# A third block of the down-projection by seven block products, in a two-layer encoder on one core

## The chip, the cores and the metric

One core of a Trainium2 chip runs the whole program. Its engines are TensorE (PE, matrix products, with its own weight loads, PEld), VectorE (DVE), ScalarE (ACT), GpSimd (POOL) and SyncE (SP), which issues the transfers. The metric is device time in microseconds; the time given is the median of three runs. A page of the profile and its trace come from one execution.

## The reference

Two layers of a streaming encoder work on 640 frames (512 of a prompt, 128 of a sample) of width 1024: a norm, an input projection, two groups of attention heads, an output projection, and then the feed-forward part that the change is about. All is float32.

```python
def swiglu(x, g, w_gate, w_up, w_down):
    n = rms_norm(x, g)
    return (jax.nn.silu(n @ w_gate) * (n @ w_up)) @ w_down

xp = xp + swiglu(xp, ffn_norm[l], w_gate[l], w_up[l], w_down[l])
...
y_prompt = rms_norm(xp, final_norm)
```

The hidden width is 2816, that is 22 tiles of 128.

## The kernel before, in words

**Products in three parts.** A float32 product is made of a high and a low part of each side: high by high, low by high and high by low, so that each product of 128 by 128 weights with 320 columns costs three matmuls (lines 1359 to 1361). Everything is held transposed, features on the partitions and the 640 frames in two halves of 320 columns: x as `xT` in 8 chunks.

**Seven products for eight.** A 2x2 block product can be made by seven block products of sums of the blocks. The kernel takes two output tiles of weights together with the two halves of frames as such blocks. Each group n has seven products x = 1 to 7; the left sides are sums of weight blocks (`left_sums`, L2481, DVE), split into a high part (`left_high`, L1879, ACT) and a low one (`left_low`, L2503, DVE) in a ring of six buffers. The order is the list `RUN` (L122). ACT works five products ahead (`HIGH_AHEAD`), DVE four (`AHEAD`): step i of DVE's loop is the sum and the low part for product i + 4, then what empties the banks of product i (`emptied`, L2551).

**The feed-forward part.** Tiles 0 to 3 of the hidden width go plainly. Tiles 4 to 21 are nine pairs: an even group n makes gate, an odd one up, so n = 0 to 17, seven products of 12 matmuls each. The down-projection sums over the hidden tiles in four blocks: 0 (tiles 0 to 3), 1, 2 and 3 (six tiles each). Blocks 1 and 2 go by block products too: four groups for each block (n = 18 to 25), seven products of 9 matmuls, 252 for a block, each group giving two chunks of `xT`. `emptied` calls `down_emptied` (L2530) for these: one addition from PSUM into `xT` for each product (L2543). The right sides are sums of hidden blocks, whose high parts ACT makes (`down_right_hi`, L1893) and whose low parts DVE makes (`down_right_lo`, L2509).

**Rows.** Blocks 0 and 3 (`ROWS_IN_PLACE`, L65) go plainly: for each of 8 output chunks d the weight tile is loaded (`load_down`, L630), split by ACT (`weight_hi`, L1471) and DVE (`weight_lo`, L2034), multiplied (`down_rows`, L1364; 36 matmuls in block 3, so 288 in all), and added into `xT` (L2715). The pairs of block 3 keep plain right sides for that (`in_rows`, L1905; `hidden_lo`, L2444). In block 3's rows a chunk is finished after each d: ACT squares it (L1469), POOL adds the square into `ssq` for the next norm (`sum_squares`, L2749), and ACT and DVE make the next layer's normed input `nh` and `nl` (L1467, L2041), or, in layer 1, `yT`.

**Between the layers** the input projection of layer 1 takes its weights in units u of 512 KB, through the same two buffers as the rows (`load`, L521). PE waits for `x_new` first (L711).

**The program's end** (L1413 to 1456): the last output chunk is made in two parts of 256 and 384 columns (`last_rows`); matmuls of one column sum `ssq` over the partitions, `y_turn` (L685) transposes `yT` tile by tile, ACT and DVE scale by the root into `yout` (L2008, L2722), and SP sends it out.

## Time and profile before

| what | us |
|---|---|
| median of 3 runs (1427.94 to 1428.9) | 1428.51 |
| the profiled execution | 1429.83 |
| its span | 1428.54 |
| PE busy in it | 1402.7 |
| rows of block 3, layer 0 | 42.38 |
| rows of block 3, layer 1, to the last data matmul | 44.89 |
| from there to the end | 8.99 |

The span runs from the first to the last record; 1.3 us of the profiled execution lie around it. A busy share is a mean over all stages; what an edit is worth is read in the stage where it stands.

### The profile page before, as it was taken

To read this page: it belongs to the slowest core of one execution; us is meant where nothing else is said; L and a number is where in the kernel's file an instruction comes from. 1 tells how busy PE (TensorE), PEld (TensorE's weight loads), DVE (VectorE), ACT (ScalarE), POOL (GpSimd) and SP (SyncE) were. 2 spreads that over 40 slices of the span, in tenths; PEclk is the share of its full clock that TensorE was granted. 3 is DMA by queue.
4 is the path that set the end of the run, shared out by engine and by line. 5 is a ranking of instruction groups with operands and counts; after the bars stand their busy time and mean duration, and the time that the engine had idled before them with its cause. 6 is when DMAs were issued, how large, how long until landed. Compare 5 with 4: busy or idle time off the path is not lost.

```text
span 1428.5 us, 24281 instructions
## 1 busy us (share of the span) xinstructions
PE 1402.7 (98%) x9340; PEld 1321.5 (93%) x9340; DVE 1061.1 (74%) x1875; ACT 713.0 (50%) x1414; POOL 156.6 (11%) x110
## 2 busy tenths in 40 slices
PE   7999999999999999999999999999999999999998
PEld 6897878999999999999988978699999999999998
DVE  5658667878789889877444776677797998998853
ACT  5458555334355455454444685643344544544534
POOL 2416020210000000000222341102000000000002
PEclk9999999999999999999999999999999999999999
DMA  5330221233022222322233211213221223222312
GB/s 171 109 113 14 74 70 39 81 104 104 30 89 66 89 84 74 104 89 74 74 84 107 85 56 47 77 42 102 79 74 60 82 71 114 62 88 89 111 45 96
DMA packets 148642, 115.25 MB, mean 81 GB/s; under 512 B 17936, under 2 KB 143248, under 8 KB 148496
## 3 DMA queue, kind: packets, MB, share of 16 engines
q1 hardware_dynamic: 148528, 113.71, 26.4%
q8 instruction: 75, 1.23, 0.4%
q14 instruction: 39, 0.32, 0.1%
HBM read 108.90 MB, written 6.62 MB: 81 GB/s over the span
## 4 chain that ended last, share of the span: by engine, by line
PE 86%; DVE 7%; ACT 3%; DMA 1%; issue 1%; SPq 1%; DVEq 0%; ACTq 0%
PE ps L675 23%; PE ps L1359 13%; PE ps L1360 13%; PE ps L1361 13%; PE ps L802 3%; PE ps L804 3%; PE ps L803 3%; PE ps L1236 1%; PE ps L1127 1%; ACT pw L1521 1%; PE ps L728 1%; DMA wraw<-w_uq 1%; DVE ringl L2507 1%; PE ps L917 1%; PE ps L1153 1%
## 5 line engine op out<-in xcount | busy, mean ns | idle before, releaser
L2037 DVE TENSOR_TENSOR wlo<-wraw,whi 128x1024 fp32r<-128x1024 f32 (+2 forms) x87 | 97.6, 1122 | 122.9 <-ACT whi L1475 122.8
L1360 PE MATMUL ps<-tl,ringh 128*128 128x320 f32 x576 | 177.8, 309 | 0.0
L1361 PE MATMUL ps<-tth,ringl 128*128 128x320 f32 x576 | 177.5, 308 | 0.0
L1359 PE MATMUL ps<-tth,ringh 128*128 128x320 f32 x576 | 177.0, 307 | 0.0
L1891 ACT ACTIVATE ringh<-sums 128x512 fp32r<-128x512 f32 (+1 forms) x208 | 123.7, 595 | 106.3 <-DVE sums L2499 35.9
L2507 DVE TENSOR_TENSOR ringl<-sums,ringh 128x512 fp32r<-128x512 f32 (+1 forms) x208 | 134.2, 645 | 9.6 <-ACT ringh L1891 8.2
L1475 ACT ACTIVATE whi<-wraw 128x1024 fp32r<-128x1024 f32 (+2 forms) x87 | 81.0, 936 | 112.5 <-PE ps L675 52.0
L1360 PE MATMUL ps<-tbl,ringh 128*128 128x320 f32 x432 | 133.5, 309 | 0.0
L1361 PE MATMUL ps<-tbh,ringl 128*128 128x320 f32 x432 | 133.4, 309 | 0.0
L1359 PE MATMUL ps<-tbh,ringh 128*128 128x320 f32 x432 | 133.4, 309 | 0.0
L1359 PE MATMUL ps<-dhi,ringh 128*128 128x320 f32 x336 | 105.6, 314 | 5.2 <-DVE dlo_rest L2512 2.8
L1359 PEld LDWEIGHTS ps<-tth,ringh 128*128 128x128 f32 x576 | 108.2, 188 | 0.0
L1361 PEld LDWEIGHTS ps<-tth,ringl 128*128 128x128 f32 x576 | 108.2, 188 | 0.0
L1360 PEld LDWEIGHTS ps<-tl,ringh 128*128 128x128 f32 x576 | 108.0, 187 | 0.0
L1361 PE MATMUL ps<-dhi,ringl 128*128 128x320 f32 x336 | 103.8, 309 | 0.0
L2755 POOL TENSOR_TENSOR ssq<-sq 128x640 f32<-128x640 f32 x4 | 6.5, 1628 | 886.1 <-ACT sq L1469 886.1
L1360 PE MATMUL ps<-dlo_rest,ringh 128*128 128x320 f32 x288 | 89.0, 309 | 0.0
L802 PE MATMUL ps<-whi,nh 128*128 128x512 f32 (+1 forms) x220 | 86.4, 393 | 0.7 <-DVE nl L2041 0.7
L804 PE MATMUL ps<-whi,nl 128*128 128x512 f32 (+1 forms) x220 | 84.0, 382 | 0.0
L803 PE MATMUL ps<-wlo,nh 128*128 128x512 f32 (+1 forms) x220 | 83.8, 381 | 0.0
L1359 PEld LDWEIGHTS ps<-tbh,ringh 128*128 128x128 f32 x432 | 81.1, 188 | 0.0
L1361 PEld LDWEIGHTS ps<-tbh,ringl 128*128 128x128 f32 x432 | 81.1, 188 | 0.0
(431 smaller groups left out, 3786.4 us busy)
## 6 DMA issues: line engine op xcount, KB each, us to landing
raw_gate<-w_gate SPq DMA_DIRECT2D x18, 1024.0 KB, 5.4
raw_up<-w_up SPq DMA_DIRECT2D x18, 1024.0 KB, 5.3
raw_gate<-w_down SPq DMA_DIRECT2D x8, 768.0 KB, 4.2
raw_up<-w_down SPq DMA_DIRECT2D x8, 768.0 KB, 4.2
wraw<-w_down SPq DMA_DIRECT2D x16, 384.0 KB, 3.3
wraw<-w_out SPq DMA_DIRECT2D x32, 128.0 KB, 2.9
wraw<-w_out SPq DMA_DIRECT2D x16, 256.0 KB, 3.1
wraw<-w_gate SPq DMA_DIRECT2D x8, 512.0 KB, 3.9
```

The source lines that it names most:

```text
L675: ins = mm(outs[j], wt[:, k, cols], x[:, half(j)], start=first and part == 0 and x is xh, stop=last and part == 1)
L728: ins = turn(ps[:, 5 + b % 3, j * P:(j + 1) * P], src, ident)
L802: mm(o, nh[:, c, tok(t)], wh[:, k, 0:w], start=c == 0, stop=False)
L803: mm(o, nh[:, c, tok(t)], wl[:, k, 0:w], start=False, stop=False)
L804: ins = mm(o, nl[:, c, tok(t)], wh[:, k, 0:w], start=False, stop=c == NC_ - 1)
L1359: mm(o, wh[:, c, :], xh[:, c, :], start=fresh and c == 0, stop=False, skip_group_check=True)
L1360: mm(o, wh[:, c, :], xl[:, c, :], start=False, stop=False, skip_group_check=True)
L1361: ins = mm(o, wl[:, c, :], xh[:, c, :], start=False, stop=c == (DP if down else KH) - 1, skip_group_check=True)
L1475: run(whi[:, unit_cols(u)], wraw[:, unit_cols(u)], ACT.Copy).then_inc(unit_hi.sem, 1)
L1891: run(ring_of(n, x)[0], left_of(n, x), ACT.Copy).then_inc(a_hi.sem, 1)
L2037: vec.tensor_tensor(wlo[:, w], wraw[:, w], whi[:, w], ALU.subtract).then_inc(unit_lo.sem, 1)
L2507: vec.tensor_tensor(lo, left_of(n, x), high, ALU.subtract).then_inc(a_lo.sem, 1)
```

## The change

In both layers block 3's down-projection goes by seven block products as well (`NDOWN` 3 x 4 groups, n = 18 to 29): 252 matmuls in place of 288. Its rows, their loads and splits, and the `in_rows` case of pairs 6 to 8 leave; those pairs make right sides like the others. The very last group (n = 29) takes its products in the order 1, 5, (28, 4), 6, 2, 7, 4, 3.

`first_rights` puts two low parts of right sides ahead of the sum and the low part in DVE's step.

ACT squares chunks in pairs at step 6 of groups 27, 28 and 29 (and makes `yT` there in layer 1), and POOL adds them there. The next layer's first two weight units have buffers of their own, in space that is free once the last gate and up group is done; the third is loaded when all products of the layer are done. `nh` and `nl` follow when the ring's buffers are free.

At the program's end, twelve turns of `yT` stand between the last products of PE; the rest of the turns and the square sums (three matmuls of one column for a tile) follow the last product.

The diff, cut to what the text speaks of:

```diff
-NDOWN = 2 * KH
+NDOWN = 3 * KH
...
-ROWS_IN_PLACE = (0, 3)
-UNITS = U_DOWN + len(ROWS_IN_PLACE) * NC_
+UNITS = U_DOWN + NC_
...
+        yield n, 2
+        yield n, 7
 
 
 def down_products(blk):
@@ -114,12 +108,11 @@
         yield n, 5
         yield (n - 1 if n > first else GROUPS_OF[blk][1] - 1), 4
         yield n, 6
-        yield n, 3
-        yield n, 2
-        yield n, 7
-
-
-RUN = [key for part in (products(1), down_products(1), products(2), down_products(2), products(3)) for key in part]
+        for x in (3, 2, 7) if n < NG + NDOWN - 1 else (2, 7, 4, 3):
+            yield n, x
+
+
+RUN = [key for part in (products(1), down_products(1), products(2), down_products(2), products(3), down_products(3)) for key in part]
...
+def row_done(d):
+
+    n = NG + 2 * KH + d // 2
+    return D_NEW[n, 4] if d % 2 else max(D_NEW[n, 2], D_NEW[n, 3])
...
+    _, next_raw, next_hi, next_lo = place(R0, [("skip_next", [P, 2560], F32), ("next_raw", [P, 2 * SLOT], F32),
+                                               ("next_hi", [P, 2 * SLOT], F32R), ("next_lo", [P, 2 * SLOT], F32R)])
...
-    yT, = place(20480, [("yT", [P, NC_, T], F32)])
+    yT, = place(R0 + 20480, [("yT", [P, NC_, T], F32)])
...
+                if l and u == 0:
+                    sp.wait_ge(a_used.sem, a_used.at(l - 1, STEP[NG - 1, 4] + 1))
+                if l and u == 2:
+                    sp.wait_ge(a_used.sem, a_used.at(l, 0))
...
-            sp.wait_ge(a_used.sem, a_used.at(l, STEP[NG + NDOWN - 1, 4] + 1))
-            for d in range(NC_):
-                load_down(3, d)
...
-            if l > 0:
-                pe.wait_ge(x_new.sem, x_new.at(l, -1))
...
+                        if l and u == 0 and k == 0 and t in (0, 3):
+                            pe.wait_ge(d_new.sem, d_new.at(l - 1, D_NEW[NG + NDOWN - 2, 4] if t == 0 else NDOWN * 7))
...
+                if l == DEPTH - 1 and n == NG + NDOWN - 1 and x == 7:
+                    pe.wait_ge(n_hi.sem, n_hi.at(DEPTH, -3))
+                    y_turn(0, range(4))
+                    pe.wait_ge(d_new.sem, d_new.at(l, D_NEW[n - 1, 4]))
+                    y_turn(1, range(4))
+                if l == DEPTH - 1 and n == NG + NDOWN - 1 and x == 4:
+                    pe.wait_ge(n_hi.sem, n_hi.at(DEPTH, -1))
+                    for t in range(2):
+                        y_turn(t, range(4, 6))
...
+            y_turn(t, range(6, 8)).then_inc(tile_turned.sem, 1)
...
+            ins = square_sums(2, t, [ssq, sq[:, 0], sq[:, 1]])
...
+        y_turn(2, range(6))
+        pe.wait_ge(n_hi.sem, n_hi.at(DEPTH, 1))
+        pe.wait_ge(y_gained.sem, 2)
+        y_turn(2, range(6, 8)).then_inc(tile_turned.sem, 1)
+        pe.wait_ge(sq_new.sem, sq_new.at(DEPTH, 3))
         for t in range(2, NT):
-            mm(ps[:, 7, 500 + t:501 + t], ssq[:, tok(t)], one, start=t == 2, stop=False, skip_group_check=True)
-        pe.wait_ge(y_gained.sem, 2)
-        y_turn(2, range(7, 8)).then_inc(tile_turned.sem, 1)
-        pe.wait_ge(sq_new.sem, sq_new.at(DEPTH, 2))
-        for t in range(2, NT):
-            ins = mm(ps[:, 7, 500 + t:501 + t], sq[:, 1, tok(t)], one, start=False, stop=True, skip_group_check=True)
+            ins = square_sums(3, t, [ssq, sq[:, 0], sq[:, 1]])
...
+            def squared(c):
+
+                act.wait_ge(d_new.sem, d_new.at(l, row_done(c)))
+                act.wait_ge(ssq_new.sem, ssq_new.at(l, 14 + adds_before(c)))
+                run(sq[:, c % 2, :], xT[:, c, :], ACT.Square).then_inc(sq_new.sem, 1)
+
+            def gained(c, cols=slice(0, T)):
+
+                act.wait_ge(d_new.sem, d_new.at(l, row_done(c)))
+                run(yT[:, c, cols], xT[:, c, cols], ACT.Copy, scale=gv[:, G_NEXT + c:G_NEXT + c + 1]).then_inc(n_hi.sem, 1)
+
+            def next_high(c):
+
+                act.wait_ge(d_new.sem, d_new.at(l, row_done(c)))
+                act.wait_ge(a_used.sem, a_used.at(l, min(len(RUN), len(RUN) - 4 + c)))
+                run(nh[:, c, :], xT[:, c, :], ACT.Copy, scale=gv[:, G_NEXT + c:G_NEXT + c + 1]).then_inc(n_hi.sem, 1)
+
+            for i, (n, x) in enumerate(RUN):
+                if i + HIGH_AHEAD < len(RUN):
+                    left_high(*RUN[i + HIGH_AHEAD])
+                elif i + HIGH_AHEAD < len(RUN) + 2 and l < DEPTH - 1:
+                    weight_hi(l + 1, i + HIGH_AHEAD - len(RUN))
+                emptied(n, x)
+                if x == 6 and n > NG + 2 * KH:
+                    for c in (2 * (n - NG - 2 * KH) - 2, 2 * (n - NG - 2 * KH) - 1):
+                        if l == DEPTH - 1:
+                            gained(c)
+                        squared(c)
+            if l < DEPTH - 1:
+                for c in range(NC_ - 1):
+                    next_high(c)
+                squared(NC_ - 2)
...
-                if g == 0 and x == 6:
-                    down_right_lo(q, 5, 3, 4, tu[:, 1:2, half(0)])
...
+            def first_rights(n, x):
+
+                if n >= NG and (n - NG) % KH == 0 and x == 6:
+                    down_right_lo(DP * ((n - NG) // KH) + DP - 1, 5, 3, 4, tu[:, 1:2, half(0)])
+                elif n < NG and n % 2 and x == 7:
+                    down_right_lo(n // 2, 1, 0, 1, tu[:, 0:1, half(0)])
...
-                    if up and not in_rows:
+                    if up:
                         dve.wait_ge(c_new.sem, c_new.at(l, C_NEW[n, 3]))
                         dve.wait_ge(silu_new.sem, silu_new.at(l, PLAIN + SILU[2 * pair, 2]))
                         chain("b12", vec.tensor_tensor(tu[:, 0, half(1)], tu[:, 0, half(1)], tg[:, 0, half(1)], ALU.mult))
@@ -2581,9 +2579,6 @@
                     if up:
                         dve.wait_ge(c_new.sem, c_new.at(l, C_NEW[n, 2]))
                         dve.wait_ge(silu_new.sem, silu_new.at(l, PLAIN + SILU[2 * pair, 2]))
-                    if up and in_rows:
-                        vec.tensor_tensor(tu[:, 0, :], tu[:, 0, :], tg[:, 0, :], ALU.mult).then_inc(h_new.sem, 1)
-                    elif up:
                         vec.tensor_tensor(tu[:, 0, half(0)], tu[:, 0, half(0)], tg[:, 0, half(0)], ALU.mult).then_inc(h_new.sem, 1)
                         chain_end("b12")
                         dve.wait_ge(h_new.sem, h_new.at(l, PLAIN + pair + 1))
@@ -2595,9 +2590,7 @@
                         else:
                             chain("t1", t1)
                 elif x == 7:
-                    if up and not in_rows:
-                        down_right_lo(pair, 1, 0, 1, tu[:, 0:1, half(0)])
...
-                    if in_rows:
-                        hidden_lo(f, tu[:, 0, :])
-                    elif not final:
+                    if not final:
                         down_right_lo(pair, 2, 1, 3, t12[:, :, :])
                     dve.wait_ge(a_used.sem, done)
                     dve.wait_ge(silu_new.sem, silu_new.at(l, PLAIN + SILU[2 * pair, 4]))
                     vec.tensor_tensor(tu[:, 1, half(0)], ps[:, bx, 0:HALF], tg[:, 1, half(0)], ALU.mult).then_inc(up_c21.sem, 1)
-                    if not in_rows:
-                        dve.wait_ge(right_new.sem, right_new.at(l, right_sums_before(pair) + 1 + final))
-                        dve.wait_ge(up_c21.sem, up_c21.at(l, pair + 1))
-                        vec.tensor_tensor(t34[:, 1, :], tu[:, 1, half(0)], t12[:, 1, :], ALU.subtract).then_inc(right_new.sem, 1)
-                elif x == 6 and not up and pair > 2 * DP:
-                    hidden_lo(f - 1, tu[:, 1, :])
+                    dve.wait_ge(right_new.sem, right_new.at(l, right_sums_before(pair) + 1 + final))
+                    dve.wait_ge(up_c21.sem, up_c21.at(l, pair + 1))
+                    vec.tensor_tensor(t34[:, 1, :], tu[:, 1, half(0)], t12[:, 1, :], ALU.subtract).then_inc(right_new.sem, 1)
...
+            def next_low(c):
+
+                dve.wait_ge(n_hi.sem, n_hi.at(l, 9 + c + 1))
+                if c < 2:
+                    dve.wait_ge(a_used.sem, a_used.at(l, len(RUN) - 2 + c))
+                low(nl[:, c, :], xT[:, c, :], gv[:, G_NEXT + c:G_NEXT + c + 1], nh[:, c, :]).then_inc(n_lo.sem, 1)
+
+            def gained_part(c, cols):
+
+                dve.wait_ge(d_new.sem, d_new.at(l, D_NEW[NG + NDOWN - 1, 4 if c == 7 else 3]))
+                vec.tensor_scalar(yT[:, c, cols], xT[:, c, cols], gv[:, G_NEXT + c:G_NEXT + c + 1], None, ALU.mult).then_inc(y_gained.sem, 1)
+
+            for i, (n, x) in enumerate(RUN):
+                first_rights(n, x)
+                if i + AHEAD < len(RUN):
+                    left_sums(*RUN[i + AHEAD])
+                    left_low(*RUN[i + AHEAD])
+                elif l < DEPTH - 1:
+                    if i + AHEAD < len(RUN) + 2:
+                        weight_lo(l + 1, i + AHEAD - len(RUN))
+                    else:
+                        next_low(i + AHEAD - len(RUN) - 2)
+                emptied(n, x)
+                if l == DEPTH - 1 and n == NG + NDOWN - 1 and x == 4:
+                    gained_part(7, slice(0, CUT))
+            if l < DEPTH - 1:
+                for c in range(2, NC_ - 1):
+                    next_low(c)
+            else:
+                gained_part(6, slice(CUT, T))
...
-            sum_squares(l, ssq, 18, 14, NC_ - 1)
+            sum_squares(l, ssq, 18, 14, NC_ - 1 if l < DEPTH - 1 else NC_ - 2)
```

## Rows read from the trace of the kernel before

**Rows 1.** Page: busy us (share of span) x instructions; PE clock in 40 slices.

```profile
PE 1402.7 (98%) x9340; PEld 1321.5 (93%) x9340; DVE 1061.1 (74%) x1875; ACT 713.0 (50%) x1414; POOL 156.6 (11%) x110
...
PEclk9999999999999999999999999999999999999999
```

**Rows 2.** Chain of waits: start, us, engine, tile, line, count.

```profile
676.86 42.23 PE ps L675 x288
...
1374.82 36.95 PE ps L675 x252
```

**Rows 3.** Windows: us; busy PE PEld DVE ACT POOL; clock, DMA share, GB/s.

```profile
448.46:492.70 44.24, 43.11 (x291) 42.23 (x290) 41.44 (x90) 19.04 (x39) 0.00 (x0) 1.00 0.31 99
...
492.70:561.23 68.53, 68.53 (x471) 68.53 (x469) 58.67 (x106) 37.51 (x73) 0.00 (x0) 1.00 0.24 75
...
561.23:606.41 45.18, 43.38 (x291) 42.24 (x289) 41.38 (x90) 19.33 (x39) 0.00 (x0) 1.00 0.31 98
...
1260.34:1304.57 44.23, 43.10 (x290) 42.22 (x289) 41.45 (x90) 19.12 (x39) 0.00 (x0) 1.00 0.31 100
```

**Rows 4.** Chain of waits, a transfer after 561.23.

```profile
573.66 6.41 DMA raw_gate<-w_down
```

**Rows 5.** Page, DMA issues: count, size, us to landing.

```profile
raw_gate<-w_down SPq DMA_DIRECT2D x8, 768.0 KB, 4.2
```

**Rows 6.** Windows of the first down stage, in two parts.

```profile
446.14:473.20 27.06, 25.93 (x173) 25.05 (x173) 26.68 (x60) 11.19 (x24) 0.00 (x0) 1.00 0.27 88
...
473.20:487.85 14.65, 14.65 (x102) 14.65 (x101) 13.29 (x30) 5.62 (x11) 0.00 (x0) 1.00 0.23 73
```

**Rows 7.** Timeline of PE: start, us, operation, [idle before <- releaser].

```profile
449.90 0.42 PE L1359 MATMUL ps<-dhi,ringh 128*128 128x320 f32 x1 [0.42 <-DVE dlo_first L2512]
...
457.98 0.41 PE L1359 MATMUL ps<-dhi,ringh 128*128 128x320 f32 x1 [0.69 <-DVE dlo_rest L2512]
```

**Rows 8.** Lines of DVE, 446:487: count | busy us, mean ns | idle.

```profile
L2543 DVE TENSOR_TENSOR xT<-ps,xT 128x320 f32<-128x320 f32 x26 | 12.6, 484 | 1.4 <-PE ps L1361 1.4
...
L2507 DVE TENSOR_TENSOR ringl<-sums,ringh 128x384 fp32r<-128x384 f32 x15 | 8.2, 550 | 0.0
```

**Rows 9.** Windows of block 3's rows in both layers, and the end.

```profile
676.70:719.08 42.38, 42.38 (x291) 42.16 (x289) 21.05 (x24) 17.55 (x23) 9.90 (x6) 1.00 0.22 63
...
1374.66:1419.55 44.89, 44.89 (x315) 44.82 (x314) 14.78 (x20) 19.65 (x28) 9.39 (x6) 1.00 0.13 36
...
1419.55:1428.54 8.99, 4.18 (x37) 3.81 (x35) 3.88 (x7) 3.03 (x6) 0.00 (x0) 0.97 0.73 292
```

**Rows 10.** Lines of ACT in layer 0's rows stage.

```profile
L1469 ACT ACTIVATE sq<-xT 128x640 f32<-128x640 f32 x7 | 5.1, 723 | 0.0
```

**Rows 11.** Timelines of POOL and DVE at two places.

```profile
716.25 1.65 POOL L2755 TENSOR_TENSOR ssq<-ssq,sq 128x640 f32<-128x640 f32 x1 [1.83 <-ACT sq L1469]
...
717.15 1.83 DVE L2037 TENSOR_TENSOR wlo<-wraw,whi 128x1024 fp32r<-128x1024 f32 x1 [0.69 <-ACT whi L1475]
...
721.80 1.23 DVE L2037 TENSOR_TENSOR wlo<-wraw,whi 128x1024 fp32r<-128x1024 f32 x1
...
282.44 1.65 POOL L2755 TENSOR_TENSOR ssq<-ssq,sq 128x640 f32<-128x640 f32 x1 [4.33 <-ACT sq L1469]
...
284.00 0.81 DVE L2433 TENSOR_TENSOR xt<-ps,rB 128x640 f32<-128x640 f32 x1
```

**Rows 12.** Timelines of the program's end, runs of one line together.

```profile
1420.36 0.83 PE L1445 MATMUL ps<-kc,ssq 128*128 128x1 f32 x6
...
1421.78 1.94 PE L689 MATMUL ps<-kc,yT 128*128 128x128 f32 x16
...
1422.47 2.07 DVE L2724 TENSOR_SCALAR yout<-ps,small 128x512 f32<-128x512 f32 x3
...
1424.61 0.33 SPq L655 DMA_DIRECT2D out_ys<-yout  x1
```

**Rows 13.** DMA issues after layer 0's rows, input weights.

```profile
wraw<-w_in SPq DMA_DIRECT2D x4, 512.0 KB, 3.6
```

More of the change, by code:

```diff
@@ L1413, in last_rows @@
-        def last_rows(right, rows):
-            wh, wl = unit_parts(UNITS - 1, P)
-            cols = slice(CUT, T) if right else slice(0, CUT)
-            out = ps[:, 6 + right, 0:cols.stop - cols.start]
-            for f in rows:
-                mm(out, wh[:, f, :], hh[:, f, cols], start=f == 0, stop=False)
-                mm(out, wh[:, f, :], hl[:, f, cols], start=False, stop=False)
-                ins = mm(out, wl[:, f, :], hh[:, f, cols], start=False, stop=f == TILES[-1] - 1)
-            return ins
@@ new lines, in _ @@
+            for n, x in RUN:
+                product(n, x)
+                if l == DEPTH - 1 and n == NG + NDOWN - 1 and x == 7:
[7 more added lines that the diff above has]
+                        y_turn(t, range(4, 6))
@@ new lines, in _ @@
+            for d in range(NC_):
+                if d == 0:
+                    right_high_sums(3)
+                if d + 6 < NC_:
+                    weight_hi(l, U_DOWN + d + 6)
+                if 2 <= d < 2 + HIGH_AHEAD:
+                    left_high(*RUN[d - 2])
+            def squared(c):
+                act.wait_ge(d_new.sem, d_new.at(l, row_done(c)))
+                act.wait_ge(ssq_new.sem, ssq_new.at(l, 14 + adds_before(c)))
+                run(sq[:, c % 2, :], xT[:, c, :], ACT.Square).then_inc(sq_new.sem, 1)
@@ L2597, in emptied @@
                 elif x == 7:
[L2598 to L2600 removed]
+                    if up and final:
                         down_right_lo(pair, 2, 1, 2, t12[:, 0:1, :])
@@ L2608, in emptied @@
                         b22 = vec.tensor_tensor(tu[:, 1, half(1)], tu[:, 1, half(1)], tg[:, 1, half(1)], ALU.mult)
-                    if up and not in_rows:
                         chain("b22", b22)
@@ new lines, in _ @@
+            weight_lo(l, U_DOWN + 2)
+            hidden_lo(PLAIN - 1, tu[:, 1, :])
+            right_low_plain(2)
+            weight_lo(l, U_DOWN + 3)
+            right_low_sums(2)
+            right_rows(3)
+            weight_lo(l, U_DOWN + 4)
+            right_sums(3)
+            weight_lo(l, U_DOWN + 5)
+            right_low_plain(3)
+            for d in range(NC_):
+                if d == 2:
+                    right_low_sums(3)
+                if d in (2, 3):
+                    weight_lo(l, U_DOWN + d + 4)
+                if 2 <= d < 2 + AHEAD:
+                    left_sums(*RUN[d - 2])
+                    left_low(*RUN[d - 2])
+                b0 = 2 * DOWN_PAIR[d]
+                dve.wait_ge(unit_used.sem, unit_used.at(l, U_DOWN + d + 1))
+                vec.tensor_tensor(halves(xT[:, d, :]), ps[:, b0:b0 + 2, 0:HALF], halves(xT[:, d, :]), ALU.add).then_inc(x_new.sem, 1)
```

278 lines of the change are left out of this document (82 added, 196 removed).

## Prediction

> **What bounds the kernel.** I read the busy times first, then the granted clock, then the chain of waits. TensorE (PE) is busy 98% of the span, with the granted clock at its upper level, 2.4 GHz, in all 40 slices [rows 1]. So a change is worth what it takes from PE's own work, less the waits that it puts before PE. In the chain the plain down-projection of block 3 is one run of PE in each layer: 42.23 us for 288 matmuls in layer 0, that is 0.1466 us for one of 320 columns; layer 1's 252 in one run take 36.95, the same each [rows 2]. The stage windows show what seven block products cost in practice. A gate and up stage of block products takes 68.53 us for its 468 matmuls, 0.1464 each: nothing waits there, though VectorE (DVE) is busy 58.67 of it. A down stage (36 matmuls of the group before, 252 of its own) takes 44.24, 45.18 and 44.23 in the three windows shown [rows 3]; 288 x 0.1465 is 42.2. So each loses 2.0 us, and 45.18 once. That 0.95 more is one late transfer, 6.41 us against the usual 4.2 [rows 4, 5].
>
> **Why a down stage loses 2 us** is seen on DVE: in its first 27 us it is busy 26.68 of 27.06, and in the next 14.65 it has 1.36 free [rows 6]. PE's stalls name it: 0.42 for dlo_first and 0.69 for dlo_rest, the low parts of the right side [rows 7]; behind each comes some 0.1 to refill. A group of seven products brings DVE 7 lows and 4 sums at 0.55 and 7 additions into xT at 0.48 [rows 8]; the sums have the shape of the lows. They overlap at their ends, so that they start some 0.47 and 0.40 apart: 11 x 0.47 + 7 x 0.40 = 8.0 of the 9.23 us that PE needs for 63 matmuls. In the rows stage that the change replaces, DVE is busy 21.05 of 42.38 [rows 9]: half free.
>
> **The method for the new stages.** Each engine takes its queue in order, so I walked the four queues operation by operation: one starts when its engine is free and its last wait is met, with the durations of the rows. For the old down stages this gives 44.1 against the 44.24 of the window: an error of 0.1 in a stage. The order stands in RUN: DVE does the sums and the low of the product four ahead, then xT for the present one.
>
> **Part 1, the products.** 36 matmuls fewer per layer: 252 x 0.1465 = 36.92 in place of 42.38, that is -5.4 before any wait. Entry to the new stage: DVE is as full as in the other two, 2.15 by the walk (2.03 measured). Pairs 6 to 8 now make right sides as the others do; block 3's gate and up stage becomes the one that waited for nothing [rows 3], so 0. On SP's queue eight loads of 384 KB leave in each layer and eight of 768 KB for two groups each come; each has the lead of the ring as now (4.2 us), so 0, and 0.95 for each that is late as in [rows 4].
>
> **Part 2, the square sums.** This is what decides. In the rows stage ScalarE squares each finished chunk (0.72) and POOL adds it into ssq (1.65) [rows 10, 11], beside a half idle DVE. Now both come in pairs inside the product stage: at step 6 of groups 27, 28 and 29, five adds in a layer. ScalarE has the room. POOL's adds are another thing: the weight low part at 717.15 took 1.83, with an add running from 716.25 for 1.65, and 1.23 right after, alone. The difference is about what was left of the add. An operation that reads PSUM, at 284.00, took its 0.81 while an add was ending [rows 11]. So I take it that an operation of DVE with both inputs in SBUF (lows, sums, weight lows) stands until the add is over, and xT, which reads PSUM, does not. The Trainium skill says this in its page "SBUF — State Buffer", section "SBUF: two separate sides": the port pair that GpSimd and DVE share is an exclusive lock for a whole instruction, against DVE operations with two SBUF inputs. By that rule the walk below holds, and without it the first rival; the row at 717.15 agrees (0.60 longer), but no row shows it with DVE full.
>
> Layer 0, by the walk with these holds: adds 1 to 3 hold lows of groups 27 to 29 for 0.95, 1.40 and 1.00; DVE's slack of 1.2 us in a group doesn't win that back, and product 4 of group 28 waits 0.93 for xT of its product 7. Adds 4 and 5 then hold the two weight lows of the next layer, 1.00 each. Those two (1.23 each) now stand in DVE's queue just before xT of product 7 of the last group, for which product 4 waits. The queue is: weight low 0, xT of product 2, weight low 1, xT of product 7; PE stands 3.58 there (1.10 without the holds). Sum: 36.92 + 2.15 + 0.93 + 3.58 + 0.2 for two refills = 43.8, against 42.38: **+1.4**. Without the holds 36.92 + 3.36 = 40.3: -2.1.
>
> Layer 1 has no weight lows there, but ScalarE makes yT there too: product 4 of group 27 waits 1.27 and of group 28 1.57 (all excess over 36.92, turns included, is 6.6; without the holds 4.4). Twelve turns of yT stand between the last products, 0.12 each by the 16 turns in 1.94 [rows 12]: 1.4. Sum to the last product's end: 36.92 + 2.15 + 1.27 + 1.57 + 0.2 + 1.4 = 43.5.
>
> **Part 3, the program's end.** Now: 8.99 from the last data matmul to the end, of which 5.06 to the last output's issue at 1424.61 and 3.93 after it [rows 9, 12]. After: xT of the last product 0.75 behind its end, square and yT of that part 0.6, then 15 one-column sums and the turns of tile 2 (six sums took 0.83) until 3.05; root and reciprocal until 3.7, three yout in 2.07, issue and transfer 3.93: **9.7**. So layer 1 from the start of the stage is 43.5 + 9.75 = 53.3 against 44.89 + 8.99 = 53.9: **-0.6**. Without holds -2.8.
>
> **Part 4, smaller steps.** first_rights puts two low parts ahead of a sum and a low in DVE's step. With DVE full this only moves which operation is late: by the walk 0 to +0.24 in each of the four old stages (the stalls of [rows 7] go, and others come at products 6 and 7, for xT). The other bound is that the stalls go: -1.1 for each. I take +0.15, the walk being within 0.1 of what is measured: **+0.6**. The next layer's first two weights have buffers of their own and come 20 us ahead: 0. The third is asked for after the last product; it lands 3.6 us later [rows 13], ScalarE and DVE need some 2.3 for it (1.23 the low part), and PE has two units of thirty 512-column matmuls first, 7 us each by 512/320 of 0.1466. So some 3 us are left when ScalarE waits for the first unit to be used: 0; without that cover it would cost what it is late. Normed chunks of the next layer: the first two lows end within 0.3 of PE's last product: 0 to +0.3, taken 0.
>
> **Sum**: +1.4 - 0.6 + 0.6 = +1.4. The profiled execution took 1429.83, 1.32 above the median of 1428.51; 0.95 of that is the late transfer, which I don't expect again. Against its own time 1429.83 - 0.95 + 1.4 = 1430.3; against the median 1429.9. I take the latter, as three runs carry it.
>
> **Rivals.** (A) The adds don't hold DVE in this stage, or fall beside xT and idle ends: -2.1 - 2.8 + 0.6 = -4.3, 1424.2. For it: the profile's durations of POOL are rough, the holds are seen at few places, and DVE has no full stage with adds in the trace. Against: 717.15. (B) Slower: the holds reach PE in full. Each of the eight adds that have two-input operations beside them (five in layer 0, three in layer 1, where the last two come after the last low) holds DVE 1.4 us, 11.2 in all, and DVE, with 1.36 free in 14.65, makes none of it up. The place is product 4 of groups 27 to 29. Layer 0: 36.92 + 3.36 + 7.0 - 42.38 = +4.9; layer 1: 36.92 + 4.4 + 4.2 + 9.75 - 53.9 = +1.4; with +0.6 it is +6.9, 1435.4. In the forecast 5.7 of the 11.2 reach PE; above 7.2 the change is slower by over 0.2%. For it: POOL may be held by DVE in turn, so that adds end later and a square waits for its buffer, and left_high stands behind it on ScalarE. (C) first_rights does remove the entry stalls, in all six stages: 6 x -1.1 in place of the +0.6, with the holds of the forecast: 1.4 - 0.6 - 6.6 = -5.8, 1422.7. Against: DVE 99% busy at entry [rows 6].
>
> **How the numbers follow.** Forecast 0.50, A 0.21, C 0.05, B 0.24. About 0.2%, 2.86 us, is what a measurement tells from no change: faster is under 1425.65, slower over 1431.37. A and C are faster (0.26), the forecast within (0.50), B slower (0.24). The range leaves out C and B's upper half: 1423.6 (A with a little less in the entries) to 1433.5 (half of B's 5.5 us on top of the forecast, and one late transfer). The forecast's own range is 1427.5 to 1432.3.
>
> **What would show it.** Right: PE in both new stages with 252 matmuls in 37 us of work and 5 to 7 us of stalls, the largest before product 4 of the last group in layer 0, released by xT; lows and weight lows of 1.4 to 2.2 us beside POOL's adds; old down stages at 44.2 to 44.5. Wrong: lows of 0.55 beside adds (A); old down stages near 43 (C); a stall before product 4 of every group of over 2 us (B); a wait of PE for the third weight unit, which I hold at 0.

## The result, and the profile after

| | us |
|---|---|
| before, median of 7 runs (1427.45 to 1428.9) | 1427.94 |
| after, median of 7 runs (1430.48 to 1435.95) | 1432.93 |
| ratio, 95% interval | 1.0037, 1.0026 to 1.0047 |
| profiled execution after | 1433.07 |
| its span | 1431.8 |

The changed kernel is 5.0 us slower, 0.35%. PE has less to do, as meant (1398.7 us busy against 1402.7 in [rows 1]), and waits more. The windows of the changed kernel show where (length; busy time of PE, PEld, DVE, ACT, POOL; granted clock; DMA share; GB/s): the first down stage of layer 0, the last of layer 0 with block 3, one old stage of layer 1, the last of layer 1, and the end.

```profile
447.12:491.44 44.32, 43.06 (x290) 42.22 (x289) 41.54 (x90) 19.29 (x39) 0.00 (x0) 1.00 0.31 100
672.65:719.16 46.51, 41.43 (x266) 40.04 (x265) 44.17 (x84) 22.91 (x42) 9.20 (x5) 0.96 0.22 73
1261.98:1306.65 44.67, 43.35 (x291) 42.23 (x289) 41.48 (x90) 19.36 (x39) 0.00 (x0) 1.00 0.31 98
1375.18:1419.91 44.73, 41.42 (x278) 39.99 (x277) 37.92 (x81) 25.58 (x49) 8.36 (x5) 1.00 0.16 52
1419.91:1431.77 11.86, 8.06 (x60) 7.66 (x57) 4.92 (x9) 4.70 (x9) 0.00 (x0) 0.84 0.56 223
```

These answer to [rows 3] and [rows 9]. The new stages start 12 matmuls (1.76 us) earlier than the rows did, since product 4 of the last up group now stands inside them. So 46.51 is to be held against 42.38 + 1.76 = 44.14, and 44.73 against 44.89 + 1.76 = 46.65. In the 42.38 of [rows 9] DVE was busy for half the time and the clock stood at 1.00; now it is busy 44.17 of 46.51, and the clock's mean is 0.96.

| part | before | after | difference | forecast |
|---|---|---|---|---|
| four old down stages, without the late transfer | 176.95 | 177.84 | +0.9 | +0.6 |
| layer 0, last stage | 44.14 | 46.51 | +2.4 | +1.4 |
| layer 1's first units (to the first turn of ssq) | 20.52 | 20.84 | +0.3 | 0 |
| layer 1, last stage | 46.65 | 44.73 | -1.9 | -1.4 |
| the end | 8.99 | 11.86 | +2.9 | +0.8 |
| sum | | | +4.5 | +1.4 |

The sum (4.5 before the parts are rounded) is near the measured 5.0. Single profiles differ in stretches that no edit here touches: in the changed kernel and its nine variants below the first down stage starts anywhere from 445.61 to 449.58. So the experiments are read by these stages first, and by their medians second.

**Layer 0's wait.** The largest wait of the new stages is before product 4 of layer 0's last group. Timelines of POOL, DVE and PE at that place (start, us, operation, and idle time before it with its releaser):

```profile
709.51 4.06 POOL L2743 TENSOR_TENSOR ssq<-ssq,sq 128x640 f32<-128x640 f32 x2 [4.80 <-ACT sq L1957]
...
709.85 2.32 DVE L2032 TENSOR_TENSOR next_lo<-next_raw,next_hi 128x1024 fp32r<-128x1024 f32 x1
712.09 0.48 DVE L2535 TENSOR_TENSOR xT<-ps,xT 128x320 f32<-128x320 f32 x1
712.49 2.16 DVE L2032 TENSOR_TENSOR next_lo<-next_raw,next_hi 128x1024 fp32r<-128x1024 f32 x1
714.58 0.48 DVE L2535 TENSOR_TENSOR xT<-ps,xT 128x320 f32<-128x320 f32 x1
...
715.11 0.64 PE L1353 MATMUL ps<-dhi,ringh 128*128 128x320 f32 x1 [3.49 <-DVE xT L2535]
715.54 0.47 PE L1354 MATMUL ps<-dlo_rest,ringh 128*128 128x320 f32 x1
```

Two adds of POOL run, and beside them the two weight lows of DVE take 2.32 and 2.16 (1.23 alone in [rows 11]), while xT between them takes its 0.48. The xT at 714.58 is the one that PE waits for. The matmul after the wait takes 0.64, the next 0.47, where 0.31 is usual: the granted clock has fallen. Windows of half a microsecond, the last column but two:

```profile
714.00:714.50 0.50, 0.00 (x0) 0.00 (x0) 0.50 (x1) 0.00 (x0) 0.00 (x0) 1.00 0.00 0
714.50:715.00 0.50, 0.00 (x0) 0.00 (x0) 0.50 (x3) 0.00 (x0) 0.00 (x0) 0.62 0.00 0
715.00:715.50 0.50, 0.39 (x1) 0.39 (x2) 0.50 (x2) 0.00 (x0) 0.00 (x0) 0.50 0.00 0
...
718.00:718.50 0.50, 0.50 (x5) 0.50 (x5) 0.50 (x2) 0.50 (x1) 0.00 (x0) 0.96 0.00 0
```

PE had stood idle since 711.6. From 714.6 to 718.0 the clock is at its lower level, 1.2 GHz, over 11 of the last 18 matmuls.

**Layer 1's waits and the end.** Product 4 of groups 27 and 28 waits 1.08 and 1.00, and the end takes PE without a gap from 1419.91 on:

```profile
1400.06 0.41 PE L1353 MATMUL ps<-dhi,ringh 128*128 128x320 f32 x1 [1.08 <-DVE xT L2535]
...
1410.58 0.41 PE L1353 MATMUL ps<-dhi,ringh 128*128 128x320 f32 x1 [1.00 <-DVE xT L2535]
...
1419.91 0.60 PE L683 MATMUL ps<-kc,yT 128*128 128x128 f32 x4
1420.35 0.28 PE L1397 MATMUL ps<-kc,ssq 128*128 128x1 f32 x2
1420.49 0.58 PE L1397 MATMUL ps<-kc,sq 128*128 128x1 f32 x4
...
1422.52 0.28 PE L1397 MATMUL ps<-kc,ssq 128*128 128x1 f32 x2
...
1424.44 3.53 PE L683 MATMUL ps<-kc,yT 128*128 128x128 f32 x16
1424.62 0.27 ACT L2018 ACTIVATE small<-ps,kc 128x3 f32<-128x3 f32 x1 [1.07 <-PE ps L1397]
...
1425.97 0.33 SPq L650 DMA_DIRECT2D out_y<-yout  x1
...
1428.84 0.33 SPq L650 DMA_DIRECT2D out_ys<-yout  x1
```

Each sum of one column is two records: the sums of tiles 2 to 4, nine of them, are 18 records from 1422.52 to 1424.44, 0.107 each and 0.214 for a sum. The root of the last three tiles comes 4.71 after the last product. The last turns run at the lower clock (3.53 for 16, against 1.94 in [rows 12]).

### The profile page after: what moved, and what is told of

Same layout as the page of the kernel before. It is cut to its first block, busy times and chain, and to the rows that moved or that the text cites. A ratio compares the mean times of both kernels' runs of the same rounds, so it can differ in the third digit from the quotient of the medians.

```text
span 1431.8 us, 24544 instructions
## 1 busy us (share of the span) xinstructions
PE 1398.7 (98%) x9278; PEld 1314.9 (92%) x9278; DVE 1124.8 (79%) x2032; ACT 732.1 (51%) x1472; POOL 157.6 (11%) x109
## 3 DMA queue, kind: packets, MB, share of 16 engines
q8 instruction: 75, 1.23, 0.4%
## 4 chain that ended last, share of the span: by engine, by line
PE 80%; DVE 12%; ACT 3%; issue 3%; DMA 1%; SPq 1%; DVEq 0%; ACTq 0%
PE ps L670 18%; PE ps L1353 13%; PE ps L1354 13%; PE ps L1355 13%; PE ps L796 3%; PE ps L798 3%; PE ps L797 3%; DVE ringl L2501 2%; DVE xT L2535 2%; PE ps L1230 1%; PE ps L1121 1%; ACT pw L1487 1%; PE ps L720 1%; PE ps L911 1%; PE ps L1147 1%
## 5 line engine op out<-in xcount | busy, mean ns | idle before, releaser
L1353 PE MATMUL ps<-dhi,ringh 128*128 128x320 f32 x504 | 159.5, 317 | 13.4 <-DVE xT L2535 13.0
L2501 DVE TENSOR_TENSOR ringl<-sums,ringh 128x512 fp32r<-128x512 f32 (+1 forms) x240 | 152.6, 636 | 7.9 <-ACT ringh L1857 6.4
L1355 PE MATMUL ps<-dhi,ringl 128*128 128x320 f32 x504 | 156.2, 310 | 0.0
L2032 DVE TENSOR_TENSOR wlo<-wraw,whi 128x1024 fp32r<-128x1024 f32 (+1 forms) x69 | 79.3, 1149 | 79.4 <-ACT whi L1442 79.3
L1354 PE MATMUL ps<-dlo_rest,ringh 128*128 128x320 f32 x432 | 133.9, 310 | 0.0
L1442 ACT ACTIVATE whi<-wraw 128x1024 fp32r<-128x1024 f32 (+1 forms) x69 | 65.8, 956 | 93.6 <-PE ps L798 38.2
L1353 PEld LDWEIGHTS ps<-dhi,ringh 128*128 128x128 f32 x504 | 95.1, 189 | 20.1 <-DVE xT L2535 19.7
L1355 PEld LDWEIGHTS ps<-dhi,ringl 128*128 128x128 f32 x504 | 95.1, 189 | 0.0
L2535 DVE TENSOR_TENSOR xT<-ps,xT 128x320 f32<-128x320 f32 x168 | 82.2, 490 | 14.9 <-PE ps L1355 14.9
L1354 PEld LDWEIGHTS ps<-dlo_rest,ringh 128*128 128x128 f32 x432 | 81.7, 189 | 0.0
```

Of the source, the lines that this page charges most:

```text
L1353: mm(o, wh[:, c, :], xh[:, c, :], start=fresh and c == 0, stop=False, skip_group_check=True)
L1354: mm(o, wh[:, c, :], xl[:, c, :], start=False, stop=False, skip_group_check=True)
L1355: ins = mm(o, wl[:, c, :], xh[:, c, :], start=False, stop=c == (DP if down else KH) - 1, skip_group_check=True)
L1442: run(high[:, unit_cols(u)], raw[:, unit_cols(u)], ACT.Copy).then_inc(unit_hi.sem, 1)
L2032: vec.tensor_tensor(lo[:, w], raw[:, w], high[:, w], ALU.subtract).then_inc(unit_lo.sem, 1)
L2501: vec.tensor_tensor(lo, left_of(n, x), high, ALU.subtract).then_inc(a_lo.sem, 1)
```

## The experiments

The theory had three parts: POOL's adds hold DVE's operations with two inputs in SBUF; in layer 0 the weight lows stand before the xT that PE waits for; and, new from the trace after, the clock falls behind that wait and at the end. The rivals: DVE's queue is simply full, with or without adds; the clock costs nothing; and the reordering of the right sides is to blame.

The kernel before was timed again beside each series: 1427.94 beside the changed kernel; 1428.42 beside the short adds, the fillers, the lows behind and the old right sides; 1427.29 beside the late squares, the pieces and the first order of the end; 1428.44 beside the last two. The changed kernel was not, so a difference from its median of about 1 us says nothing.

### The adds cut short

```diff
-                first = sq[:, 0, :] if c == 1 else into[:, :]
-                add(into[:, :], first, sq[:, c % 2, :], ALU.add).then_inc(ssq_new.sem, 1)
+                w = slice(0, 8 if squares_before == 18 else T)
+                first = sq[:, 0, w] if c == 1 else into[:, w]
+                add(into[:, w], first, sq[:, c % 2, w], ALU.add).then_inc(ssq_new.sem, 1)
```

> The changed kernel with POOL's adds of squares in the last product stage cut from 640 columns to 8, so that sums of squares are left out for most columns; every wait stands as it was. Theory (an add of POOL holds DVE's operations with two inputs in SBUF): DVE's weight lows take 1.23 in place of 2.2 to 2.3; the wait before product 4 of the last group in layer 0 falls from 3.65 to about 1.1 us and the clock stays up; layer 1's waits before product 4 of groups 27 and 28 (1.24 and 1.16) mostly go. Layer 0 about 4 us less, layer 1 about 2: 1427. Rival (DVE's queue is full by itself): the waits stay, 1433.

This kernel leaves out most of the sums of squares. Measured: 1426.70 (11 runs), 0.9985 of before (0.9977 to 0.9994) and 6.2 us under the changed kernel. Windows of the two last stages and of the end:

```profile
671.53:713.58 42.05, 39.80 (x266) 38.70 (x265) 39.45 (x84) 23.18 (x42) 1.40 (x5) 1.00 0.23 79
1369.95:1412.61 42.66, 41.41 (x278) 40.00 (x277) 35.86 (x81) 25.55 (x49) 1.13 (x5) 1.00 0.17 55
1412.61:1424.47 11.86, 6.47 (x60) 6.24 (x57) 4.73 (x9) 4.58 (x9) 0.00 (x0) 0.90 0.56 223
```

DVE at the same place as above, and PE's wait:

```profile
707.64 1.22 DVE L2032 TENSOR_TENSOR next_lo<-next_raw,next_hi 128x1024 fp32r<-128x1024 f32 x1
708.77 0.48 DVE L2535 TENSOR_TENSOR xT<-ps,xT 128x320 f32<-128x320 f32 x1
709.17 1.21 DVE L2032 TENSOR_TENSOR next_lo<-next_raw,next_hi 128x1024 fp32r<-128x1024 f32 x1
...
710.84 0.41 PE L1353 MATMUL ps<-dhi,ringh 128*128 128x320 f32 x1 [1.01 <-DVE xT L2535]
```

The weight lows take 1.22 and 1.21. Layer 0's last stage loses 4.46 us, layer 1's 2.07, and the clock stays at 1.00 in both. So the adds, not a queue that is full anyway, cost 6.5 us in the changed kernel, a part of it by way of the clock (the next experiment); only about 1 us of the wait in layer 0 is the queue's own. This is the size of rival A of the prediction in both layers (-2.1 for the first stage: 42.05 against 44.14; for layer 1's, 41.3 worked out without the holds and 42.66 - 1.76 = 40.9 measured). The end is as long as in the changed kernel, 11.86.

### The clock: PE kept at work

```diff
+            def filler(bank, count):
+                key = (NG + NDOWN - 1, 3)
+                pe.wait_ge(a_lo.sem, a_lo.at(l, STEP[key] + 1))
+                for _ in range(count):
+                    mm(ps[:, bank, 0:HALF], ring_of(*key)[0][:, 0, :], dhi[:, RIGHT_OF[3], 0, :], start=True, stop=True, skip_group_check=True)
...
+                if l < DEPTH - 1 and n == NG + NDOWN - 1 and x == 7:
+                    filler(7, 24)
...
         pe.wait_ge(sq_new.sem, sq_new.at(DEPTH, 3))
+        filler(3, 4)
```

> The changed kernel with 24 filler matmuls of 320 columns into an unused bank ahead of the wait of product 4 of the last group in layer 0, and 4 fillers ahead of the last square sums at the program's end. Their results are read by nothing. Theory (the granted clock): the trace after shows the clock at 0.50 behind PE's wait of 3.65 us in layer 0 (714.6 to 718.1) and from 1424.6 at the end, where the last 16 turns take 3.53 us against 1.94 before. With PE at work in both places it stays at 1.00: layer 0's last products take 2.6 us in place of 4.0 (1.1 less to the next layer's start), the turns about 2.0 (1.6 less, 0.6 more for the fillers themselves). In all 2 us less than the changed kernel, 1431. Rival (the clock falls whatever PE does there, or costs nothing): the same 3.5 us of turns, and 0.6 more, 1433.5.

Measured: 1432.81 (7 runs), ratio 1.0033 (1.0022 to 1.0044): as the changed kernel. The places tell more than the sum. PE in layer 0:

```profile
710.38 3.68 PE L1386 MATMUL ps<-dhi,ringh 128*128 128x320 f32 x24
714.06 0.41 PE L1353 MATMUL ps<-dhi,ringh 128*128 128x320 f32 x1
714.31 0.31 PE L1354 MATMUL ps<-dlo_rest,ringh 128*128 128x320 f32 x1
```

Windows of layer 0's last stage, of the end, and of the last turns within it:

```profile
671.51:716.81 45.30, 43.64 (x291) 42.26 (x290) 44.12 (x84) 22.86 (x42) 9.23 (x5) 1.00 0.22 74
...
1418.56:1431.03 12.47, 7.07 (x64) 6.83 (x62) 4.73 (x9) 4.58 (x9) 0.00 (x0) 0.90 0.54 212
1423.50:1425.00 1.50, 1.50 (x15) 1.50 (x16) 0.81 (x2) 0.90 (x3) 0.00 (x0) 1.00 1.02 407
```

In layer 0 the fillers fill the wait, the clock stays at 1.00, and the stage is 1.2 us shorter than the changed kernel's 46.51, as expected (1.1). At the end the clock stays up as well through the last turns (1423.5 to 1425.0), yet the end takes 12.47 in place of 11.86: the 0.6 of the four fillers is paid, and nothing comes back for the clock. The short adds settle the end without fillers: there the clock is at 1.00 until PE's last turn is over, and the end takes the same 11.86. So the fall of the clock costs 1.2 us in layer 0 and nothing at the end. In this profile layer 1's last stage was 45.98 against 44.73, through a longer wait before product 4 of group 28; why it differs from execution to execution was not settled.

### The weight lows behind

```diff
-                    if i + AHEAD < len(RUN) + 2:
-                        weight_lo(l + 1, i + AHEAD - len(RUN))
-                    else:
-                        next_low(i + AHEAD - len(RUN) - 2)
+                    if i == len(RUN) - 2:
+                        weight_lo(l + 1, 0)
+                    if i >= len(RUN) - 2:
+                        next_low(i - len(RUN) + 2)
                 emptied(n, x)
...
             if l < DEPTH - 1:
+                weight_lo(l + 1, 1)
                 for c in range(2, NC_ - 1):
                     next_low(c)
```

> The changed kernel with the next layer's two weight lows moved in DVE's queue: the first behind xT of product 7 of the last group, the second behind the last xT. The adds stay. Theory (what PE waits for is the order of DVE's queue, lengthened by the adds): product 4 of the last group waits under 0.5 us, the clock stays up; the first weight low is then late for the next layer by up to 1.5 us, as it and two lows of the normed chunks stand before PE's next start. In all 3 us less, 1430. Rival (what is won comes back at the next layer's start, with PE waiting there 4 us or more): 1433 or above.

Measured: 1430.45 (11 runs), 1.0012 (1.0003 to 1.0020), 2.5 under the changed kernel. Layer 0's last stage:

```profile
673.53:715.75 42.22, 40.12 (x266) 38.72 (x265) 40.71 (x82) 22.85 (x42) 8.39 (x5) 1.00 0.23 79
```

DVE's first weight low, and what PE waits before product 4:

```profile
712.86 1.80 DVE L2032 TENSOR_TENSOR next_lo<-next_raw,next_hi 128x1024 fp32r<-128x1024 f32 x1
...
713.00 0.42 PE L1353 MATMUL ps<-dhi,ringh 128*128 128x320 f32 x1 [0.58 <-DVE xT L2535]
```

The adds still run, the first low is still held (1.80), but xT is ahead of it: 0.58 of waiting, no fall of the clock, 4.3 us less in the stage. Some 0.3 comes back in the next layer's first unit, where PE waits for a low. Of the 4.0 that are left the median shows 2.5, or 3.0 when each kernel is held against the kernel before of its own series; the rest was not found. What PE waited for was the order; the adds made it long.

### The squares late

```diff
-                if x == 6 and n > NG + 2 * KH:
+                if l == DEPTH - 1 and x == 6 and n > NG + 2 * KH:
                     for c in (2 * (n - NG - 2 * KH) - 2, 2 * (n - NG - 2 * KH) - 1):
...
                 for c in range(NC_ - 1):
                     next_high(c)
-                squared(NC_ - 2)
+                for c in range(NC_ - 1):
+                    squared(c)
```

> The changed kernel with layer 0's squares and POOL's adds behind the last product and the normed chunks, instead of in the product stage; layer 1 stays. Theory (the adds hold DVE in the full stage): layer 0's last stage takes about 42 us in place of 46.5, as with the short adds (42.05), with a wait of 1.2 before product 4 of the last group and the clock at 1.00; layer 1 as in the changed kernel. In all 1428.5. Rival (the holds only move: the adds then hold the lows of the normed chunks, and PE waits in the next layer's first units): 4 us come back there, 1432.5.

Measured: 1433.44 (6 runs), 1.0038 (1.0025 to 1.0051): nothing gained. The stage:

```profile
674.98:717.04 42.06, 39.81 (x267) 38.70 (x265) 39.28 (x84) 19.87 (x36) 0.00 (x0) 1.00 0.23 80
```

ACT, and then PE, in the next layer's first units:

```profile
729.16 0.74 ACT L1957 ACTIVATE sq<-xT 128x640 f32<-128x640 f32 x1 [0.98 <-POOL ssq L2744]
...
731.46 1.99 ACT L1442 ACTIVATE whi<-wraw 128x1024 fp32r<-128x1024 f32 x2
...
734.07 0.50 PE L796 MATMUL ps<-whi,nh 128*128 128x512 f32 x1 [2.87 <-DVE wlo L2033]
```

The stage has the 42.06 of the theory. The rival's time came true by another way than it named: on ACT the squares wait for the adds, two buffers for seven squares, and the third weight unit's high part stands behind them until 731.46; its low part then runs beside POOL's next add. PE waits 2.87 and the clock falls again. What a step waits for moves with it, and so does what is queued behind it.

### The right sides where they were

```diff
-                first_rights(n, x)
...
+                if g == 0 and x == 6:
+                    down_right_lo(q, 5, 3, 4, tu[:, 1:2, half(0)])
                 dve.wait_ge(a_used.sem, a_used.at(l, STEP[n, x] + 1))
...
                 elif x == 7:
+                    if up:
+                        down_right_lo(pair, 1, 0, 1, tu[:, 0:1, half(0)])
```

> The changed kernel with the two low parts of right sides where they were in the kernel before (behind the sum and the low part of DVE's step). Theory (moving them only moves the wait, with DVE full): the stages of blocks 1 and 2 at 44.24 as before in place of 44.3 to 44.7, the entry of block 3's stage alike: 0.6 to 1 us less, 1432. Rival (the move removes the entry waits and something else lengthens these stages): 1 us more for each of six stages, up to 1439.

Measured: 1433.36 (8 runs), 1.0031 (1.0020 to 1.0042): not to be told from the changed kernel. Windows of an old stage in each layer:

```profile
447.67:491.90 44.23, 43.12 (x290) 42.24 (x289) 41.43 (x90) 19.41 (x39) 0.00 (x0) 1.00 0.31 101
1264.64:1308.88 44.24, 43.13 (x290) 42.24 (x289) 41.44 (x90) 19.01 (x39) 0.00 (x0) 1.00 0.31 99
```

44.23 and 44.24 as before, against 44.32 with the reordering: 0.08 for a stage, a half of my 0.15, and far from the -1.1 of rival C. The stages of 44.67 to 44.82 that either order has hold a wait for a late transfer (5.80 us in the changed kernel's chain of waits, at 1274.50; 6.06 and 6.05 here, at 572.86 and 1163.92); the changed kernel's 44.53 has no such transfer in its chain, and its 0.2 more was not explained.

### The adds in pieces, and then everything

The pieces are of 128 columns, so that one fits beside an xT of DVE.

```diff
-                first = sq[:, 0, :] if c == 1 else into[:, :]
-                add(into[:, :], first, sq[:, c % 2, :], ALU.add).then_inc(ssq_new.sem, 1)
+                for t in range(NT if squares_before == 18 else 1):
+                    w = tok(t) if squares_before == 18 else slice(0, T)
+                    first = sq[:, 0, w] if c == 1 else into[:, w]
+                    ins = add(into[:, w], first, sq[:, c % 2, w], ALU.add)
+                ins.then_inc(ssq_new.sem, 1)
```

> The changed kernel with each of POOL's adds in the last product stage cut into five of 128 columns, one after the other. A short add of 8 columns took 0.20 us and one of 640 takes 1.65, so a piece takes about 0.48, little more than an xT (0.40 from start to start), which reads PSUM. Theory (POOL and DVE exclude each other for one instruction at a time): a piece runs under an xT and holds the next low by 0.1 only; the wait before product 4 of layer 0's last group falls from 3.65 to about 1.5, layer 1's two waits from 2.4 to about 1 together: 1428 to 1429.5. Rival (what counts is POOL's time in all, 2.4 us for an add in pieces): the waits stay or grow, 1433 to 1436.

Measured: 1429.39 (11 runs), 1.0012 (1.0003 to 1.0021). Layer 0's last stage:

```profile
672.93:716.09 43.16, 39.88 (x267) 38.73 (x266) 42.20 (x84) 23.09 (x42) 16.16 (x25) 1.00 0.23 78
```

DVE's first weight low, and PE's wait before product 4 of the last group:

```profile
709.57 1.50 DVE L2032 TENSOR_TENSOR next_lo<-next_raw,next_hi 128x1024 fp32r<-128x1024 f32 x1
...
713.34 0.42 PE L1353 MATMUL ps<-dhi,ringh 128*128 128x320 f32 x1 [2.06 <-DVE xT L2535]
```

POOL works 16.2 us in place of 9.2 for the same sums, and the stage is 3.35 us shorter, some 1.2 of it because the clock no longer falls. Here it is the length of one add that counts, not POOL's time in all. In layer 1 it is less plain: its last stage takes 44.36 against 44.73, so the pieces gave back 0.4 of the 2.1 that the short adds gave, and product 4 of groups 27 and 28 still waits 0.57 and 0.86. Why so much less was not followed up. With the weight lows behind as well:

> The changed kernel with POOL's adds in five pieces and, in layer 0, the two weight lows behind the xT that PE waits for. In pieces alone the wait before product 4 of layer 0's last group was 2.2 us, and each weight low took 1.5 there. Theory (the order of DVE's queue and the holds each cost their part of that wait): it falls under 0.5, layer 0's last stage from 43.2 to about 41.8; the next layer's start may wait some 0.4 for its first low. In all 1428.3. Rival (what was won there comes back at the next layer's start): 1429.4.

Measured: 1429.07 (11 runs), 1.0006 (0.9997 to 1.0014); the stage 41.70, as expected, the sum between theory and rival.

```profile
672.21:713.91 41.70, 39.90 (x267) 38.75 (x266) 40.23 (x83) 23.08 (x42) 15.33 (x25) 1.00 0.24 81
```

### The end in another order

First only the sums of tiles 2 to 4 ahead of tile 2's turns:

```diff
         pe.wait_ge(d_new.sem, d_new.at(DEPTH, 0))
-        y_turn(2, range(6))
-        pe.wait_ge(n_hi.sem, n_hi.at(DEPTH, 1))
-        pe.wait_ge(y_gained.sem, 2)
-        y_turn(2, range(6, 8)).then_inc(tile_turned.sem, 1)
         pe.wait_ge(sq_new.sem, sq_new.at(DEPTH, 3))
         for t in range(2, NT):
             ins = square_sums(3, t, [ssq, sq[:, 0], sq[:, 1]])
         ins.then_inc(stat_sum.sem, 1)
+        y_turn(2, range(6))
+        pe.wait_ge(n_hi.sem, n_hi.at(DEPTH, 1))
+        pe.wait_ge(y_gained.sem, 2)
+        y_turn(2, range(6, 8)).then_inc(tile_turned.sem, 1)
```

> The changed kernel with the square sums of tiles 2 to 4 ahead of tile 2's turns at the program's end. The trace after shows PE at work without a gap from the last product's end (1419.91) to 1424.44, and the root of the last three tiles at 1424.62. Theory (PE's one-column sums and turns set the end): the root comes 0.9 earlier, yout of tile 2 waits for its turns until 0.5 earlier than now, and the end is 0.5 earlier: 1432.4. Rival (the output transfers set the end, as they move some 400 GB/s from 1424.0 on): nothing changes, 1432.9.

Measured: 1434.97 (5 runs), 1.0050 (1.0038 to 1.0062). The end is 11.60 in place of 11.86, so the order is worth 0.3; the total is nevertheless the highest of all. In the profile 0.8 us more than in the changed kernel lie in layer 0's last stage, behind a longer fall of the clock (0.94 in place of 0.96), and 1.7 in layer 1 before the feed-forward part:

```profile
671.71:719.06 47.35, 42.33 (x267) 40.95 (x265) 44.12 (x84) 22.85 (x42) 9.18 (x5) 0.94 0.21 71
```

Nothing was changed in either place, so I take the median for that scatter and not for the edit. The run after holds this edit too, and is not slow. The same with the sums of tiles 0 and 1 ahead of their turns too, and the pieces and the lows of the run before:

> The same with the program's end in another order: the square sums of tiles 0 and 1 ahead of their last turns, and those of tiles 2 to 4 ahead of tile 2's turns. Theory (the end is a row of output transfers that starts when the first two tiles are scaled): the root of tiles 0 and 1 comes 0.44 earlier, and the row of transfers with it, from 11.9 us behind the last product's end to about 11.4: 1427.8, that is the time of the kernel before. Rival (transfers or the later tiles set the end whatever starts earlier): 1428.3, as without.

Measured: 1428.26 (12 runs) against 1428.44 for the kernel before in the same series: 1.0001 (0.9993 to 1.0010). Layer 0's last stage takes 41.72. Windows of layer 1's last stage and of the end:

```profile
1369.61:1413.97 44.36, 41.69 (x279) 40.02 (x277) 37.55 (x81) 25.54 (x49) 12.55 (x25) 1.00 0.16 52
1413.97:1425.46 11.49, 6.47 (x60) 6.23 (x58) 4.92 (x9) 4.70 (x9) 0.00 (x0) 0.89 0.58 230
```

SP's issue of tile 2's output:

```profile
1419.64 0.33 SPq L650 DMA_DIRECT2D out_y<-yout  x1
```

The end is 0.37 shorter, near the 11.4 that was expected, but not for the reason that I gave; the total can't tell the theory's 1427.8 from the rival's 1428.3. In five kernels the time from the issue of tile 2's output to the end of the span is the same: 1425.97 to 1431.77 (5.8) after, 1425.21 to 1431.03 (5.8) with the fillers, 1418.67 to 1424.47 (5.8) with the short adds, 1419.64 to 1425.46 (5.8) here, and 5.9 with the first order alone. The last output's issue doesn't matter in the same way: it comes 2.9 us before the end after (1428.84) and 4.4 with the short adds (1420.10). The first two tiles' outputs went 0.44 earlier here and at the same time in the others, and the first order alone, without that, had 11.60 already. So the last three outputs set the end, from the issue of the first of them, which the square sums of tiles 2 to 4 hold back; the turns at the lower clock fall beside these transfers, which is why the clock costs nothing there.

No version that makes all the sums was faster than the kernel before. What this last one still pays is waits of 0.57 and 0.86 us in layer 1 before product 4 of groups 27 and 28, and an end 2.5 us longer than before's 8.99 [rows 9].

## Why the prediction was right or wrong

The forecast was +1.4 and 1429.9; measured are +5.0 and 1432.93. That lies inside the range, 0.6 from its upper end, outside the forecast's own 1427.5 to 1432.3, on the slower side, which had 0.24. The sign of the likeliest case was right, and the mechanism of the waits too; the size was not. That the range holds it is luck in part: its upper end stood for half of rival B and a late transfer, and what filled it was the program's end and the clock.

**Right: the adds hold DVE.** The place, the operations held and the ones spared are as forecast: weight lows of 2.32 and 2.16 beside adds, 1.22 without, xT at 0.48 in both. The three earlier adds of layer 0 hold a low, a low and a sum for 1.07, 0.87 and 0.98 (1.62, 1.42 and 1.53 in place of 0.55), where 0.95, 1.40 and 1.00 were worked out. The page "SBUF — State Buffer" of the Trainium skill, section "SBUF: two separate sides", was the rule behind it; the trace agrees with its exclusive lock, and the pieces, beside which a weight low takes 1.5 in place of 2.2 to 2.3, agree with a lock that is held for one instruction at a time. Rival A falls with the short adds: what it would give is there only when the adds are gone.

**Right: the waits.** Before product 4 of layer 0's last group 3.58 was worked out and 3.49 and a refill measured; with short adds 1.10 and 1.01; in layer 1 1.27 and 1.57 against 1.08 and 1.00. The smaller one in layer 0, before product 4 of group 28, was put at 0.93 and is 0.36:

```profile
706.05 0.42 PE L1353 MATMUL ps<-dhi,ringh 128*128 128x320 f32 x1 [0.36 <-DVE xT L2535]
```

Layer 1's stage to the last product is 42.97 without the 12 matmuls, where 43.5 was forecast. Rival B, all holds reaching PE, falls with that: PE pays 6.5 us of stage and clock in all, not the 11.2.

**Wrong: the clock was left out.** Layer 0's stage was to lose 1.4 and lost 2.4. The sum 36.92 + 2.15 + 0.93 + 3.58 + 0.2 has the wait of 3.5 us as a wait alone; behind it the clock stood at its lower level for 3.4 us, and the fillers show that this cost 1.2.

**Wrong: the end, the largest miss.** 9.75 was forecast, 11.86 measured: 2.1 of the 3.6 by which the whole sum was missed. The step that failed is "15 one-column sums and the turns of tile 2 (six sums took 0.83) until 3.05". The row in [rows 12] counts six records, and a sum has two: 0.83 is three sums. By start to start a sum costs 0.214, so that 15 sums take 3.2 in place of 2.1; and the four turns of tiles 0 and 1 ahead of them (0.44, from 1419.91 to 1420.35) are not in the 3.05. The sums and turns end at 4.53, the root of the last three tiles comes at 4.71, and tile 2's output is issued at 6.06, where the sum had it at some 4.5 (3.7 and a first yout of 0.75). The other 0.5 lies behind that issue: from it to the end are 5.8, and 5.25 in the kernel before (1423.29 to 1428.54), from which the 3.93 behind the last issue was taken.

**Small terms.** The old stages were given +0.6: the reordering itself costs 0.08 each, 0.3, and the other 0.6 lie in two stages of that execution, 0.35 of it in the one with the late transfer. The next layer's first units were taken at 0 with 0.3 as the bound, and 0.3 it was. The third weight unit was in time, as forecast; it was late only where the squares were put before it.

**Open.** The changed kernel's runs spread over 5.5 us; those of the kernel before over 1.5 in the same series and 6.0 in a later one of 23, so the spread is not the change's alone. The waits of layer 1 differ between executions of the same order (1.00 and 1.85 before product 4 of group 28), which is part of it. Layer 0's clock differs too: in two other profiles in which this wait is as it was (the old right sides and the first order of the end) the lower level lasts 6.8 us in place of 3.4, and the stage takes 47.27 and 47.35 in place of 46.51, so that the fall costs some 2.0 there. The rest of the scatter lies in stretches that the edits don't touch, and was not explained.

## What to carry to other kernels

Before work is moved into a stage, ask which engine is full there: 36 matmuls fewer, 5.3 us of PE, gave 2.1 us in layer 0's stage even with the adds cut short, as the engine that feeds them has 0.9 us free in ten. Work on an engine that looks idle can still cost, if it shares something with the full one; cutting it into pieces gave 3.4 of 4.5 us back in one stage, and 0.4 of 2.1 in the other. A wait of PE of some microseconds costs more than its length if the clock falls behind it, and the length of this program's end is read from the issue of the first of its last transfers, not of the last.
